# Layer two's expert blocks fed from the residual on chip, and their results summed in PSUM

## What is computed

```python
h2 = modulate(rmsnorm(x, g_ffn[l]), mod[:, 3, None], mod[:, 4, None])   # h * (1 + scale) + shift
...
combine = ...          # each token: 2 of 16 experts, weights that sum to 1
for e in range(N_EXPERTS):
    he = (silu(h @ w1[e]) * (h @ w3[e])) @ w2[e]
    out = out + combine[:, e:e + 1] * he
...
x = x + mod[:, 5, None] * y
return rmsnorm(x, g_final)
```

## Time and profile before

| what | value |
|---|---|
| median of 3 runs | 1142.3 us (1140.0 to 1145.42) |
| the profiled execution | 1148.53 us, its span 1146.7 us |
| mean granted TensorE clock | 0.900 |
| busy: PE, DVE, ACT, POOL | 81%, 39%, 22%, 20% of the span |
| moved by DMA | 317.45 MB, mean 277 GB/s |
| read from and written to DRAM | 308.62 MB and 12.65 MB |
| indirect gathers and scatters, both layers | 68 and 64 |

### The profile page before, as it was taken

How to read it: one execution, slowest core, us unless ns; L and a number is a source line. 1 busy time by engine, 2 the same in 40 slices (tenths; PEclk the granted TensorE clock), 3 DMA queues, 4 the chain that set the end, 5 groups by cost and what they waited for, 6 DMA issues and landing times. The chain is left out here.

```text
span 1146.7 us, 23528 instructions
## 1 busy us (share of the span) xinstructions
PE 924.9 (81%) x8592; PEld 545.5 (48%) x8593; DVE 448.7 (39%) x1049; ACT 248.4 (22%) x491; POOL 227.0 (20%) x375
## 2 busy tenths in 40 slices
PE   3999999988897599979779399999896577555871
PEld 3546446455454356646446166544653344322440
DVE  2187515654554323323222566426633322111223
ACT  2100111543321122313122030124421112111110
POOL 4100000110020144425333220001000133211231
PEclk9999999989988699989899699999897689877886
DMA  9998601820004989999999977128206899999993
GB/s 348 380 413 299 245 3 71 339 93 1 1 19 159 374 316 405 422 416 417 422 420 411 388 288 283 74 74 340 110 1 225 323 413 398 417 428 426 417 379 117
DMA packets 54014, 317.45 MB, mean 277 GB/s; under 512 B 7288, under 2 KB 8008, under 8 KB 35136
## 3 DMA queue, kind: packets, MB, share of 16 engines
q1 hardware_dynamic: 41168, 286.21, 62.1%
q0 software_dynamic: 9584, 20.02, 4.9%
q10 hardware_dynamic: 3200, 10.36, 2.4%
HBM read 308.62 MB, written 12.65 MB: 280 GB/s over the span
## 5 line engine op out<-in xcount | busy, mean ns | idle before, releaser
L1923 PE MATMUL ps<-ring,area 128*32 128x256 f32 x3808 | 243.5, 407 | 63.6 <-DMA ring<-in_w 38.5
L1923 PE MATMUL ps<-ring,HT 128*128 128x512 f32 (+1 forms) x576 | 259.1, 603 | 2.3 <-ACT HT L1164 1.5
L1923 PE MATMUL ps<-area 128*32 128x256 f32 (+3 forms) x1928 | 225.3, 399 | 20.9 <-DVE area L1821 9.7
L1923 PEld LDWEIGHTS ps<-ring,area 128*32 128x32 f32 x3808 | 142.1, 117 | 154.3 <-issue 49.8
L1923 PEld LDWEIGHTS ps<-ring,HT 128*128 128x128 f32 x576 | 110.4, 197 | 128.7 <-issue 126.5
L1923 PEld LDWEIGHTS ps<-area 128*32 128x32 f32 (+2 forms) x1928 | 129.7, 139 | 45.4 <-issue 25.3
L1923 PE MATMUL ps<-HT,area 128*32 128x256 f32 x704 | 93.9, 426 | 40.9 <-DMA area<-in_w 32.3
L971 POOL DMA_INDIRECT expert_rows<-area x64 | 69.0, 1079 | 248.9 <-DVE area L1871 111.2
L1844 DVE STREAM_TRANSPOSE area<-area 128x256 f32<-128x256 f32 x65 | 29.0, 446 | 226.0 <-PE ps L1923 225.7
L1217 ACT ACTIVATE area<-ps 128x128 f32<-128x128 f32 x63 | 17.5, 278 | 362.7 <-PE ps L1923 362.7
L961 POOL DMA_INDIRECT area<-h_rows,area x68 | 71.3, 1048 | 100.4 <-DVEq L1834 42.4
(11 more groups left out here) (221 smaller groups left out, 734.5 us busy)
## 6 DMA issues: line engine op xcount, KB each, us to landing
ring<-in_w SPq DMA_DIRECT2D x64, 2048.0 KB, 10.2
ring<-in_w_ada SPq DMA_DIRECT2D x24, 2048.0 KB, 18.7
area<-in_w SPq DMA_DIRECT2D x21, 1024.0 KB, 11.2
ring<-in_w_in SPq DMA_DIRECT2D x10, 2048.0 KB, 16.3
HT<-in_w SPq DMA_DIRECT2D x10, 2048.0 KB
area<-in_w SPq DMA_DIRECT2D x10, 2048.0 KB, 10.5
ring<-in_w_out SPq DMA_DIRECT2D x4, 2048.0 KB, 8.4
area<-expert_rows ACTq DMA_DIRECT2D x12, 512.0 KB, 5.2
```

Source lines behind the costliest of these rows:

```text
L1923: return t_.matmul(out, lhsT, rhs, start=first, stop=last_)
```

## The change

In layer two nothing of the tokens goes through DRAM any more. The router's normalised rows are not made; instead:

- `choose(n)` (DVE) makes, for block n, a 128 x 32 matrix for each of the two tiles of tokens that picks a slot's token and carries its 1/rms (from `PC1` and `OC`, which the router now leaves behind).
- `token_rows(n)` (TensorE, 8 products) multiplies it with the residual X into bank 0; `scale_x` (DVE) transposes the block out of PSUM and multiplies by gain x (1 + scale), which `F2` now holds as columns; `shift_x` adds the shift and writes `xT`.
- `gated_y(m)` (DVE) compares a row of token numbers (`TOK1`, one load of 128 KB) with the slot's token to get a 128 x 256 choice matrix `oht`, and writes `ym`.
- `add_rows(m)` (TensorE, 8 products of 32 rows by 128 columns of the array, 256 columns moving) adds the block into banks 4 to 7, where all blocks of layer two are summed. In the first block four products with a zero matrix, 512 columns each, clear these banks.
- After the last block DVE adds the banks to X (two additions of 128 x 1024) and the final norm follows.

Gone from layer two: both `make_h2`, the two stores of h2, all gathers and scatters, the reads of `YA` and `YB`, POOL's part of the blocks, and one of two barriers. SP's three waits at the down piece of expert 2 become one, for the scaled logits, and its wait at the first piece of expert 3 is for X, no more for h2. Three broadcast loads of 512 KB become three of 4 KB. In both layers the rows of the up weights are stored in another order (p = row // 8), and the 32x32 transposes read their source with a step of 8 elements. The diff, cut:

```diff
@@ load_expert (SP)
-                            sp.wait_ge(pl_done, l + 1)
-                            sp.wait_ge(h2_out[l], 16 * (routed(l) // P))
-                            sp.wait_ge(gath[l][0], 16)
+                            sp.wait_ge(u_done[l], 1)
+                            if not last:
+                                sp.wait_ge(pl_done, l + 1)
+                                sp.wait_ge(h2_out, 16 * TILES)
+                                sp.wait_ge(gath[0], 16)
@@ routing (DVE)
+                    if l:
+                        v.tensor_tensor(OC[:, k * nq:(k + 1) * nq], CO[:, k * nq:(k + 1) * nq], rstd[:, 0:nq].unsqueeze(2).to_broadcast([P, nq, CB]), ALU.mult)
...
@@ the blocks of layer two (DVE)
-                    v.transpose(xT, xs).then_inc(xt_rdy[l], 1)
+                    v.transpose(xT.rearrange("p (k s) -> p k s", k=KD), xs.rearrange("p (f k) -> p k f", k=KD)).then_inc(xt_rdy[l], 1)
+                def choose(n):
+                    v.tensor_tensor(oh4, PC1[:, :, 0:SLOT], OC[:, :, bass.ds(n, 1)].to_broadcast([P, 4, SLOT]), ALU.mult)
+                    dve.drain()
+                    v.tensor_tensor(ohb, oh4[:, 0:2], oh4[:, 2:4], ALU.add).then_inc(oh_rdy, 1)
+                def scale_x(n):
+                    hold(dve, xg_full, n + 1, dve_passed)
+                    v.transpose(xr.rearrange("p (k s) -> p k s", k=KD), ps[:, B_XG, 0:NW].rearrange("p (f k) -> p k f", k=KD))
+                    dve.drain()
+                    v.tensor_tensor(xm.rearrange("p (k s) -> p k s", k=KD), xr.rearrange("p (k s) -> p k s", k=KD),
+                                    F2[:, 1].unsqueeze(2).to_broadcast([P, KD, SLOT]), ALU.mult)
+                def shift_x(n):
+                    if not isinstance(n, int) or n:
+                        hold(dve, w13_full[l], n, dve_passed)
+                    v.tensor_tensor(xT.rearrange("p (k s) -> p k s", k=KD), xm.rearrange("p (k s) -> p k s", k=KD),
+                                    F2[:, 0].unsqueeze(2).to_broadcast([P, KD, SLOT]), ALU.add).then_inc(xt_rdy[l], 1)
+                def gated_y(m, ended=False):
+                    if ended:
+                        hold(dve, w2_full[l], m + 1, dve_passed)
+                    v.tensor_scalar(oht, TOK1, TK[:, bass.ds(m, 1)], None, ALU.is_equal)
+                    if not ended:
+                        hold(dve, w2_full[l], m + 1, dve_passed)
+                    v.tensor_tensor(ym[:, 0:NW], ps[:, B_W2, 0:NW], G4, ALU.mult).then_inc(y_rdy[l], 1)
+                def own_step(b):
+                    shift_x(b + 1)
+                    hold(dve, si_rdy[l], b + 1, dve_passed)
+                    v.scalar_tensor_tensor(gg, sg, TW[:, bass.ds(b, 1)], ps[:, B_W13, P:2 * P], ALU.mult, ALU.mult).then_inc(g_rdy[l], 1)
+                    if not isinstance(b, int):
+                        gated_y(b - 1)
+                    dve.drain()
+                    v.transpose(gT, gg).then_inc(gt_rdy[l], 1)
+                    scale_x(b + 2)
+                    choose(b + 3)
...
+                    dve.wait_ge(acc_full, 1)
+                    for i in range(nq):
+                        added = ps[:, B_ACC:B_ACC + NG, i * NW:(i + 1) * NW]
+                        v.tensor_tensor(X[:, i].rearrange("p (a n) -> p a n", a=NG), X[:, i].rearrange("p (a n) -> p a n", a=NG), added, ALU.add).then_inc(comb[l], 1)
@@ the blocks of layer two (TensorE)
+                def token_rows(n):
+                    hold(pe, oh_rdy, n + 1, pe_passed)
+                    for i in range(nq):
+                        for j in range(NG):
+                            last = mm(ps[SLOT * j:SLOT * (j + 1), B_XG, 0:NW], ohb[:, i], X[:, i, j * NW:(j + 1) * NW], i == 0, i == nq - 1)
+                    last.then_inc(xg_full, 1)
+                def add_rows(m, stop=False):
+                    hold(pe, y_rdy[l], m + 2, pe_passed)
+                    for i in range(nq):
+                        for j in range(NG):
+                            last = mm(ps[:, B_ACC + j, i * NW:(i + 1) * NW], oht[SLOT * j:SLOT * (j + 1), i * P:(i + 1) * P],
+                                      ym[SLOT * j:SLOT * (j + 1), 0:NW], False, stop and i == nq - 1)
+                    return last
@@ step (TensorE), behind the down product of block b-1
+                    if l:
+                        token_rows(b + 2)
+                        if first:
+                            for h in range(4):
+                                mm(ps[:, B_ACC + h], oht[:, 0:P], cst[:, 0:CHUNK], True, False)
+                        else:
+                            add_rows(b - 1)
```

More of the change, by code:

```diff
@@ L584, in hybrid_moe_kernel @@
         nb_ready = sem("counts_ready")
-        gath = [sems(f"tokens_gathered_{l}", 2) for l in range(DEPTH)]
-        xs_rdy = sems("tokens_copied", DEPTH)
+        gath = sems("tokens_gathered", 2)
+        xs_rdy = sem("tokens_copied")
         xt_rdy = sems("xT_copied", DEPTH)
@@ L594, in hybrid_moe_kernel @@
         spare_in = sem("spare_half_in")
-        scat = [sems(f"y_scattered_{l}", 2) for l in range(DEPTH)]
+        scat = sems("y_scattered", 2)
         dve_passed = sem("dve_waits_passed")
@@ L1203, in _ @@
                         columns(st_[1])
[L1204 removed]
+                        if l == 0 and st_[1] < nq - 1:
                             store_h2(st_[1])
@@ L1688, in _ @@
                         scaled_logits(h)
-                make_h2(nq - 1)
+                if l == 0:
+                    make_h2(nq - 1)
                 for i in range(max(nq - 2, 0), nq):
@@ new lines, in _ @@
+                if l:
+                    v.memset(oht, 0.0)
+                    choose(0)
+                    scale_x(0)
+                    choose(1)
+                    dve.drain()
+                    shift_x(0)
+                    scale_x(1)
+                    choose(2)
+                    dve.drain()
+                    dve.wait_ge(tok1_in, 16)
+                    dve.wait_ge(gate2_in, 32 + 16 * NG)
+                    own_step(0)
+                    copied = dve.alloc_register("dve_own_blocks")
+                    dve.reg_mov(copied, 0)
+                    with dve.Fori(1, blocks) as b:
+                        own_step(b)
+                        dve.reg_add(copied, copied, 1)
+                    gated_y(dve.snap(copied), True)
+                    dve.wait_ge(acc_full, 1)
+                    for i in range(nq):
+                        added = ps[:, B_ACC:B_ACC + NG, i * NW:(i + 1) * NW]
+                        v.tensor_tensor(X[:, i].rearrange("p (a n) -> p a n", a=NG), X[:, i].rearrange("p (a n) -> p a n", a=NG), added, ALU.add).then_inc(comb[l], 1)
+                    dve.wait_ge(fin_g, 16)
+                    for i in range(2):
+                        dve.wait_ge(rs_done, TILES * DEPTH + i + 1)
+                        for half in (slice(0, D // 2), slice(D // 2, D)):
+                            v.scalar_tensor_tensor(X[:, i, half], X[:, i, half], rstd[:, i:i + 1], GFIN[:, half], ALU.mult, ALU.mult).then_inc(fin_o, 1)
+                    barrier(dve, bar(l, 6))
+                    return
@@ L2342, in expert @@
                             step(sl, sl[2], None, up=up)
+                if l:
+                    token_rows(0)
+                    token_rows(1)
                 expert(0, 0, 0, True)
```

216 lines of the change are left out of this document (124 added, 92 removed).

## The result

Over 20 runs each, the kernel after took 1148.85 us in the median (1140.35 to 1153.63), the kernel before 1145.49 (1140.0 to 1148.85): a ratio of 1.0033, with a 95% interval of 1.0018 to 1.0048. That is slower by a third of a per cent, inside the 0.5% called no change, and on the other side of the forecast. The range held the time. The median of before rose from 1142.3 (three runs) to 1145.5 with more runs, so 3.2 us of the 9.9 between forecast and result are the base that was carried over.

What follows compares the result with a forecast made beforehand. The weight stream was taken to set the pace. Last block +3.7, tail +0.4 and -7.4 gave -3.3 us on the 1146.7 span, 1143.4, carried over to the median as 1139.0 us; range 1128 to 1155.

Steps and rivals of the forecast that it cites:

- What leaves the stream: Layer two's weight stream: without 26 gathers and 23 scatters a piece takes 4.94 us, 0.34 us won on each.
- The head: Layer two's start: token products and clearing products make the second up product begin 3.5 us late.
- A block: Each layer-two block on TensorE: two row-product groups and hand-overs add 2.2 us, bounds 1.8 and 4.8.
- hand-overs of 0.4: Within a block on TensorE: two shape changes at 0.1 each and some 0.2 of exposed loop work.
- change of shape: TensorE switching array layout around the row products: 0.1 us for each of two changes a block.
- rows one behind the other: Rival, in blocks: `add_rows` 3.5 us, a block 4.8 more, 1178 us; chance 0.16, shared with stalls over 3.2 a block.
- The chain to the end: Experts 2 to 15: expert 12's up pieces arrive 5.3 us earlier, but the last block is 3.7 us later.
- Places come back just in time: Experts 2 to 6: nine blocks, 74 us, match 15 weight pieces, also 74, so buffers free in time.
- The tail: Behind the last up product: 0.4 us more to last `ym`, then 7.4 won; 12.1 remain to the end.
- half clock: Rival, TensorE's clock around expert 12: full speed wins 3.2 us; with lighter blocks 1134.4 us; chance 0.25 together.
- It doesn't give the stream back: Rival, weight stream: the 0.34 us a piece is nothing; +5.5 us, 1147.8 us; chance 0.07.
- Half an overlap: Rival, in blocks: `add_rows` takes 2.0 us, adding 1.1 in nine places; +6.6 us, 1149; no chance of its own given.

Runs made afterwards that it cites:

- d_norows: Kernel after without the row products in layer two's loop (output of other data): 1142.12 us, ratio 0.9983 to before.
- c_clear: Kernel after without the four clearing products behind the first up product: 1149.7 us, ratio 1.0045 to before.
- b_branch: Kernel after with the loop over further blocks left out for experts 0 and 1: 1144.21 us, ratio 0.9998 to before.
- n_two: Kernel after with an early GpSimd drain and without the further-block loops of experts 0 and 1: 1141.02 us, ratio 0.9927 to before.
- e_add: Kernel after with each block's row addition moved behind the next block's up product: 1146.98 us, ratio 1.0032 to before.
- i_all: Kernel after with later row addition, early GpSimd drain and no further-block loops for experts 0 and 1: 1136.42 us, ratio 0.9945 to before.
- f_drain: Kernel after with one more GpSimd drain, early, behind the router's roots in layer two: 1141.12 us, ratio 0.9995 to before.
- g_before_drain: Kernel before with one more GpSimd drain, behind its last wait for a scatter: 1142.85 us, ratio 0.9988 to before.
- k_drains: Kernel after with GpSimd drains behind layer one's last scatter, behind layer two's router roots and at the end: 10.28, 2.40 and 1.06 us; no total given.
- a_end: Kernel after with GpSimd's drain ahead of the last barrier taken out: 1154.65 us, ratio 1.0091 to before.

## Why the prediction was wrong

**What leaves the stream: right.** 4.89 us a piece where nothing holds it, 4.94 forecast; and d_norows gave the stream's gain back up to expert 12.

**The head: right in its terms.** Clearing 3.70 us, as forecast; `token_rows` 1.05 instead of 0.9; the second up product 2.1 us late instead of 3.5, as the first one ran partly at full clock (4.48 us instead of 6.07; granted clock 0.81 from 899.8 to 904.4, where the earlier trace rows have 0.50). What the terms missed is that the first branch's 2.4 us lie under the clearing products, so that taking these out gains nothing while the branch is there (c_clear).

**A block: right, a little high.** 1.82 us against 2.2. `add_rows` takes 1.15 us for 16 products on four row tiles: one behind the other at 0.22 each they would take 3.5, so these do run side by side. The hand-overs of 0.4 do not show: the addition begins at 915.55, as the token product ends (914.55 + 1.07). So the change of shape between the two, 0.1 in the forecast, cost nothing that can be read here. The rival of rows one behind the other fell with that.

**The chain to the end: here it failed.** "Places come back just in time", and expert 12's up pieces "arrive 5.3 earlier": its product ended 0.9 later. The step weighed experts 2 to 6 as 74 us of blocks against 74 us of pieces. The blocks were sized right (73.4 us from expert 2's first silu to expert 7's in after). But the weighing let TensorE come to expert 2 in time, and put at nothing what lies ahead of that: expert 1's block, which is longer too, and the gap behind it. From the first silu, the third up product began 5.7 us later than before (16.53 against 10.83), 3.2 of it from the head and 2.5 from expert 1's block. The gap was no new one, 4.25 us against 4.27; what changed is its price. The load that needs a place of expert 1 waited for it 0.8 us in before, 4.9 in after and under 0.1 in b_branch. Before, TensorE stood waiting for weights soon after (48.9 us in all); in after TensorE was the late one, and the stream waited for it.

How the 6.2 us divide between the gap and the longer blocks is open. In the profiles, taking the branches out is worth 2.0 us up to expert 12 (b_branch; 1.8 in n_two), the later addition nothing (e_add), both together 6.6 (i_all), about what the stream by itself allows (6.8, d_norows); but the times don't bear out the step from n_two to i_all, and f_drain, whose stall was shorter by chance (2.64 us), came 3.6 earlier with the additions in place.

**The tail: right, its end wrong.** 6.89 and 1.77 us against 6.6 and 1.9. But "from there 12.1 us remain to the end" took the rest as fixed. It was not: before, GpSimd's drain already ended 2.6 us behind the stores; after, with a longer drain (11.04 us against 7.21) and the rest earlier, 6.4 behind them, and f_drain takes just that away. Without this and the branches of experts 0 and 1 the change comes out ahead: n_two is 0.7% under before. That is not quite a fair match, since before has both costs too. Its drain alone is worth little (g_before_drain); what its branch is worth was not tried.

**The rivals.** The half clock stayed: expert 12's gap shrank from 8.02 to 5.12 us, as this rival said, and its up product still took 6.43 against 6.57 (granted clock 0.50 from 1059 to 1065). No run shows the 3.2 us at which it priced the clock; from its first instruction to its silu, expert 2's first up product took 3.72 us in b_branch (granted clock 1.00) and 5.93 in after (0.50 from 921 to 924). "It doesn't give the stream back" was nearest in its sum (+5.5 forecast, +4.3 measured), but for another reason than the one given: the pieces were faster, and waited for places. "Half an overlap" was nearest in time (1149 against 1148.85) by luck alone, since `add_rows` took 1.15 us and not 2.0. None of the signs named for a wrong forecast came: `add_rows` took under 2 us, TensorE did not wait ahead of it in the loop, and the last expert's weights were there. They watched the products, and the loss lay in the queues.

## What to carry to other kernels

When a change moves the pace from one engine to another, list the idle gaps that the second engine already has, and first those that no other engine ended (`issue` here): branches, drains and register work do not stand in a busy-time view. A gap can be covered while the engine has slack and cost time once it has none: here the stalls behind experts 0 and 1 lasted 6.5 us (2.40 and 4.12), and after without them was some 4.0 us faster by the ratios (b_branch). Take the end of a span as a race like any other: see which engine reaches the last barrier last, and whether that engine owes something that it could pay early, where it is idle (here GpSimd's drain: f_drain took 6.4 us off the end). And where two queues are weighed as just even, forecast the case in which they are not, since a few microseconds of lateness can stay where neither side has slack (here 6.2 up to expert 12).

## What was not expected of the hardware

- The first drain of GpSimd behind its indirect transfers took 10.0 to 10.3 us (5.8 to 6.2 behind layer two's in before and its variants), if the time that a root was still running is taken off: 0.98 of the 11.04 in after, 0.60 of f_drain's first 10.66. The last drain took 1.05 to 1.06 in f_drain, g_before_drain and k_drains, of which the root has 0.98; the one between in k_drains took 2.40, of which a root has 0.60. In after and its variants the long one was the first behind layer one's indirect transfers wherever that stood: at the barrier (11.04, after), behind the router (10.66, f_drain) or in the program's own end (10.04, a_end).
- TensorE's branch over a loop with one block's products (128 with as many weight loads) stalled 2.4 to 6.3 us behind experts 0 and 1, in all eight profiles of after and its variants that keep it. In before and its two variants, whose loops have 96, it took 0.37 us behind expert 0 and 2.3 to 3.6 behind expert 1, and in d_norows, with 96 too, 0.34 to 0.37. So the length of the loop alone doesn't decide it, and the same code gave 2.64 (f_drain) and 6.32 us (k_drains). The DMA records show what goes with the stall. They have queues of the kind `instruction`; in after, this line is the share of one such queue while the branch behind expert 1 lasts (packets, MB, share of 16 engines; 915.66 to 919.79 us):

```profile
q8 instruction: 1, 0.02, 1.5%
```

  It is one packet of 16,384 bytes, from 917.48 to 918.44, and the branch ends 1.35 us behind it. In all 16 profiles each of TensorE's branches of over 1.5 us in this stage has just one such packet landing within it, 1.34 to 1.50 us before its end, and none of those of 0.2 to 1.5 us has one. In the stall of 5.93 us in c_clear the packet starts 3.6 us into the branch, in the 4.12 us of after 1.8; why it starts late is open. That the branch waits for what this packet brings is my inference from these times; no run tests it. In the loop over the experts the branch behind expert 4, the loop's first pass, took 0.60 us in after, without such a packet, and up to 3.71 in its variants, with one in each of over 1.5; from expert 7 on it took 0.21 to 0.23 in after.
